# Branch merge and output projection on 1024 result rows, with split one-pass products in place of fp32 products

## The chip, the cores and the metric

The kernel runs on one core of a Trainium2 chip. The metric is the device time of one execution in microseconds (us); lower is better. Matrix products run on TensorE (PE), which has a weight load (PEld) beside the product proper; elementwise work runs on VectorE (DVE) and ScalarE (ACT), indirect transfers are issued by GpSimd (POOL), most plain transfers by SyncE (SP).

## The reference

One transformer-like layer over 16 meta rows and 1024 sequence rows (1040 rows, width 1024). Both branches run over all 1040 rows, but the output is `h[:, N_META:]`, so behind the branches only 1024 rows count:

```python
y_rwkv = rwkv7_time_mix(...) @ w_branch_rwkv[l]
y_diff = diff_attention(...) @ w_branch_diff[l]        # its rows are normed and scaled by subln_w * 0.8
merged = gates[..., :D_MODEL] * y_rwkv + gates[..., D_MODEL:] * y_diff
h = h + merged @ w_out[l]
u2 = rms_norm(h, norm2_w[l]).reshape(-1, D_MODEL)
h = h + hierarchical_moe(u2, ...)                      # 2 of 32 experts for each row
return h[:, N_META:]
```

All data is fp32.

## The kernel before, in words

The program is a row of stages with a barrier of all engines between them: norm, projections (`project_features`, `project_heads`), attention, `rwkv`, `merge_branches`, `output_and_route`, `dispatch`, `experts`, `combine`. The two projections split each fp32 operand into a high part (a rounding to the one-pass type fp32r, written by ACT) and a low part (the rest, written by DVE) and add three products, high by high, high by low and low by high. The stages behind rwkv use plain fp32 products.

`merge_branches` first loads the attention result in ten tiles of 104 rows (`mb_o`, lines 1422 and 1427), scales each twice on DVE (1460, 1461), transposes it on PE (1482) and copies it to `mb_oT` on ACT (1441). The rwkv result comes transposed from memory in one transfer (`mb_yT`, 1423). Only when all ten tiles are copied do the products start: 8 blocks of 128 output features times 2 branches, which makes 16 units of 8 row blocks k by 4 column groups of 260, 32 products each (1493). DVE gates each unit from PSUM (1467) and adds the two branches into `mT` (1471). SP loads each unit's weights (1431) and gates (1433) while the unit before it runs.

`output_and_route` loads all of `w_out` (1532), then `x` rows, the router's weights and the norm weights, and PE waits for all of them together. Then come ten tiles of 104 rows: 16 products of 512 columns (1578), and behind each tile the routing of the tile before it: transposes (1561), a copy on ACT (1608), 8 small products (1568). ACT's copy stands behind the square and the root of the current tile in ACT's program. `dispatch` ranks the rows per expert on DVE and scatters row numbers into slots with 20 indirect transfers (1700). `experts` runs 32 experts of 128 slots each. `combine` handles ten tiles: load `h`, two gathers, two DVE steps, one store.

Order on each engine is program order; engines meet by semaphores, each wait of which is written by hand.

Of the kernel before, what the change touches and what calls it, by code (L numbers as in the profile page):

```python
# [7 lines left out]
F32 = mybir.dt.float32  # L8
# [9 lines left out]
TT = 104  # L18
# [1364 lines left out]
OVER = 2 * T // (SLOTS + 1)  # L1383
NBLK = NE + OVER
BIG = 1.0e30


def merge_branches(nc, c):

    with ExitStack() as st:  # L1390
        sb, ps, sem, begin = scope(nc, st)
        yT = sb("mb_yT", [128, KD, T])
        oT = sb("mb_oT", [128, KD, T])
        o = sb("mb_o", [TT, 2, D])
        rs = sb("mb_rs", [TT, NT * DH])
        ri = sb("mb_ri", [TT, NT * DH])
        sw = sb("mb_sw", [TT, 128])
        w = sb("mb_w", [128, 2, KD, 128])
        gt = sb("mb_gt", [128, 2, T])
        part = sb("mb_part", [128, 2, T])  # L1400
        bank = ps("mb_bank", [128, 8, 512])
        sw_in = sem("mb_sw_in")
        o_in = [sem(f"mb_o_in{s}") for s in range(2)]
        y_in = sem("mb_y_in")
        w_in = [sem(f"mb_w_in{s}") for s in range(2)]
        g_in = [sem(f"mb_g_in{s}") for s in range(2)]
        rs_done = sem("mb_rs_done")
        vec = sem("mb_vec")
        turned = sem("mb_turned")
        moved = sem("mb_moved")  # L1410
        product = [sem(f"mb_product{s}") for s in range(2)]
        opened = [sem(f"mb_opened{s}") for s in range(2)]
        gated = [sem(f"mb_gated{s}") for s in range(2)]
        summed = sem("mb_summed")
        block = begin()
        LAMBDA0 = 0.8 - 0.6

        @block.sync
        def _(sp):
            sp.dma_start(sw[:], c.diff_subln_w.to_broadcast([TT, 128])).then_inc(sw_in, 16)  # L1420
            for t in range(2):
                sp.dma_start(o[:, t, :], c.oD[t]).then_inc(o_in[t], 16)
            sp.dma_start(yT[:], c.yrT.rearrange("f p t -> p f t")).then_inc(y_in, 16)
            with sp.Fori(1, NT // 2) as i:
                for s in range(2):
                    sp.wait_ge(turned, 2 * i + s - 1 + OPEN)
                    sp.dma_start(o[:, s, :], c.oD[bass.ds(2 * i + s, 1)].rearrange("o p d -> (o p) d")).then_inc(o_in[s], 16)
            with sp.Fori(0, KD) as i:
                for s, src in enumerate((c.w_branch_rwkv, c.w_branch_diff)):
                    sp.wait_ge(product[s], i + OPEN)  # L1430
                    sp.dma_start(w[:, s], src.rearrange("o (k p) f -> p (o k) f", p=128)[:, :, bass.ds(i * 128, 128)]).then_inc(w_in[s], 16)
                    sp.wait_ge(gated[s], i + OPEN)
                    sp.dma_start(gt[:, s, :], c.pT[bass.ds(i + RT + 8 * s, 1)].rearrange("o p t -> (o p) t")).then_inc(g_in[s], 16)

        @block.scalar
        def _(act):
            nc.scalar.activation(rs[:], c.o_ms[:].rearrange("p t h -> p (t h)"), ACT.Sqrt, bias=c.eps[0:TT, :],
                                 scale=1.0 / 128).then_inc(rs_done, 1)
            with act.Fori(0, NT) as i:
                act.wait_ge(turned, i + 1 + OPEN)  # L1440
                nc.scalar.copy(oT[:, :, bass.ds(i * TT, TT)].rearrange("p (b k) t -> p b k t", b=2),
                               bank[:, 0:2, 0:4 * TT].rearrange("p b (k t) -> p b k t", k=4)).then_inc(moved, 1)
            with act.Fori(0, KD) as i:
                for s in range(2):
                    act.wait_ge(g_in[s], 16 * i + 16 + OPEN)
                    nc.scalar.activation(gt[:, s, :], gt[:, s, :], ACT.Sigmoid).then_inc(opened[s], 1)

        @block.vector
        def _(dve):
            dve.wait_ge(sw_in, 16 + OPEN)  # L1450
            dve.wait_ge(rs_done, 1 + OPEN)
            ch = Chain(dve, vec)
            ch(nc.vector.tensor_scalar(sw[:], sw[:], 1.0 - LAMBDA0, None, ALU.mult))
            ch(nc.vector.reciprocal(ri[:], rs[:]))
            with dve.Fori(0, NT // 2) as i:
                ch = Chain(dve, vec, 4 * i + 2)
                for s in range(2):
                    dve.wait_ge(o_in[s], 16 * i + 16 + OPEN)
                    o3 = o[:, s, :].rearrange("p (h d) -> p h d", h=DH)
                    ch(nc.vector.tensor_tensor(o3, o3, ri[:, bass.ds((2 * i + s) * DH, DH)].unsqueeze(2).to_broadcast([TT, DH, 128]), ALU.mult))  # L1460
                    ch(nc.vector.tensor_tensor(o3, o3, sw[:].unsqueeze(1).to_broadcast([TT, DH, 128]), ALU.mult))
            split = lambda x: x.rearrange("p (n t) -> p n t", n=NCOL)
            with dve.Fori(0, KD) as i:
                for s in range(2):
                    dve.wait_ge(product[s], i + 1 + OPEN)
                    dve.wait_ge(opened[s], i + 1 + OPEN)
                    nc.vector.tensor_tensor(split(part[:, s, :]), bank[:, 4 * s:4 * s + 4, 0:CW], split(gt[:, s, :]),
                                            ALU.mult).then_inc(gated[s], 1)
                dve.wait_ge(gated[0], i + 1 + OPEN)
                dve.wait_ge(gated[1], i + 1 + OPEN)  # L1470
                nc.vector.tensor_tensor(c.mT[:, bass.ds(i, 1), :].rearrange("p o t -> p (o t)"), part[:, 0, :], part[:, 1, :],
                                        ALU.add).then_inc(summed, 1)
                dve.wait_ge(summed, i + 1 + OPEN)

        @block.tensor
        def _(pe):
            with pe.Fori(0, NT // 2) as i:
                for s in range(2):
                    pe.wait_ge(vec, 4 * i + 2 * s + 4 + OPEN)
                    pe.wait_ge(moved, 2 * i + s + OPEN)  # L1480
                    for k in range(KD):
                        last = nc.tensor.transpose(bank[:, k // 4, (k % 4) * TT:(k % 4 + 1) * TT],
                                                   o[:, s, k * 128:(k + 1) * 128], c.ident[0:TT, 0:TT])
                    last.then_inc(turned, 1)
            pe.wait_ge(moved, NT + OPEN)
            pe.wait_ge(y_in, 16 + OPEN)
            with pe.Fori(0, KD) as i:
                for s, src in enumerate((yT, oT)):
                    pe.wait_ge(w_in[s], 16 * i + 16 + OPEN)
                    pe.wait_ge(gated[s], i + OPEN)  # L1490
                    for k in range(KD):
                        for n in range(NCOL):
                            last = nc.tensor.matmul(bank[:, 4 * s + n, 0:CW], w[:, s, k, :], src[:, k, n * CW:(n + 1) * CW],
                                                    start=(k == 0), stop=(k == KD - 1))
                    last.then_inc(product[s], 1)


def output_and_route(nc, c):

    NR = NG + NE  # L1500
    with ExitStack() as st:
# [29 lines left out]
        def _(sp):  # L1531
# [17 lines left out]
            for s in range(2):  # L1549
                sp.wait_ge(h_out[s], 16 * NT // 2 + OPEN)  # L1550
                sp.wait_ge(u_out[s], 16 * NT // 2 + OPEN)
# [668 lines left out]
```

## Time and profile before

| | us |
|---|---|
| median of 3 runs | 4256.5 (4249.66 to 4256.95) |
| profiled execution, first to last instruction (its span; no other time is given for it) | 4243.3 |
| merge: SP's first transfer of the stage to its first of the next | 288.2 |
| output and route: from there to the last routing copy | 229.0 |
| dispatch, up to the experts' first gather | 64 |
| experts | 740 |
| combine | 82 |

These five stages follow one another behind 2840 us of earlier stages, which the change leaves alone, so what one stage loses or gains goes to the span in full. TensorE is busy 82% of the span; its granted clock is 0.900 of full on average.

### The profile page before, as it was taken

How to read it: one execution, taken by the hardware profiler on the slowest of the kernel's cores; microseconds unless marked ns; L12 is line 12 of the kernel's file. 1: busy time of each engine (PE TensorE's matmuls, PEld its weight loads, DVE VectorE, ACT ScalarE, POOL GpSimd, SP SyncE). 2: the span in 40 equal slices, each digit the busy share in tenths (PEclk: the TensorE clock that was granted, in tenths of full speed). 3: DMA queues.
4: the chain of work that ended last, by engine and by line, in shares of the span. 5: the costliest groups of instructions: out<-in, count | busy, mean ns of one | idle time of the engine just before them, and what ended most of it. 6: DMA issues, size and time to landing. Idle time of an engine off the chain costs nothing. (4 is left out here: it accounts for less than half of the span.)

```text
span 4243.3 us, 55444 instructions
## 1 busy us (share of the span) xinstructions
PE 3497.8 (82%) x20377; PEld 2677.2 (63%) x20378; DVE 1476.5 (35%) x2604; ACT 1048.2 (25%) x2216; POOL 310.3 (7%) x346
## 2 busy tenths in 40 slices
PE   2999969887777739989989989958978569999990
PEld 2999966665554528888878888846844334444440
DVE  3111123311556555656556556452111200000002
ACT  3111112212444424334334334321101001111110
POOL 0000002210000020110010011010000020000001
PEclk9999989998898869989989889878989779999995
DMA  3322221212111010000000000012222448888866
GB/s 102 126 93 91 94 101 41 80 38 56 40 28 35 25 40 9 23 17 7 23 17 7 23 17 13 16 63 84 80 83 62 160 162 334 327 343 337 323 264 165
DMA packets 154135, 419.32 MB, mean 99 GB/s; under 512 B 14445, under 2 KB 95447, under 8 KB 141663
## 3 DMA queue, kind: packets, MB, share of 16 engines
q1 hardware_dynamic: 119146, 331.21, 22.1%
q10 hardware_dynamic: 25620, 60.39, 3.8%
q0 software_dynamic: 9184, 25.36, 2.0%
q8 instruction: 105, 1.72, 0.2%
q14 instruction: 80, 0.65, 0.0%
HBM read 335.33 MB, written 81.58 MB: 98 GB/s over the span
## 5 line engine op out<-in xcount | busy, mean ns | idle before, releaser
L565 PE MATMUL at_S<-at_k,at_q 128*104 128x512 f32 (+10 forms) x544 | 202.9, 494 | 33.9 <-DMA at_v<-s_v 18.3
L1922 PE MATMUL ex_bank<-wd,ex_hT 128*128 128x512 f32 x512 | 227.8, 598 | 1.4 <-ACT ex_hT L1965 1.4
L1898 PE MATMUL ex_bank<-wgu,ex_xT 128*128 128x512 f32 x512 | 226.7, 596 | 0.0
L236 PE MATMUL pf_acc<-uH,pf_wH 128*128 128x260 f32 x1344 | 216.5, 283 | 12.1 <-DVE pf_wL L254 12.1
L1906 PE MATMUL ex_bank<-wgu,ex_xT 128*128 128x512 f32 x512 | 225.0, 593 | 0.0
L345 PE MATMUL ph_acc<-ph_wH,uH 128*104 128x512 f32 x480 | 196.9, 410 | 26.7 <-DVE ph_wL L356 26.7
L236 PE MATMUL pf_acc<-uH,pf_wL 128*128 128x260 f32 x1344 | 217.3, 284 | 0.0
L236 PE MATMUL pf_acc<-uL,pf_wH 128*128 128x260 f32 x1344 | 216.4, 283 | 0.0
L345 PE MATMUL ph_acc<-ph_wL,uH 128*104 128x512 f32 x480 | 193.3, 403 | 0.0
L236 PEld LDWEIGHTS pf_acc<-uH,pf_wH 128*128 128x128 f32 x1344 | 185.4, 190 | 12.4 <-issue 12.4
L345 PE MATMUL ph_acc<-ph_wH,uL 128*104 128x512 f32 x480 | 192.5, 401 | 0.0
L236 PEld LDWEIGHTS pf_acc<-uH,pf_wL 128*128 128x128 f32 x1344 | 185.4, 189 | 0.0
L236 PEld LDWEIGHTS pf_acc<-uL,pf_wH 128*128 128x128 f32 x1344 | 183.8, 189 | 0.0
L1971 DVE COPY ex_y<-ex_bank 128x512 f32<-128x512 f32 x32 | 22.1, 692 | 457.8 <-PE ex_bank L1922 457.8
L938 PE MATMUL rw_bank<-rw_kr,rw_bkz 128*104 128x208 f32 x640 | 143.3, 372 | 41.5 <-DVE rw_Pend L1341 25.7
L1578 PE MATMUL or_bank<-or_wo,mT 128*104 128x512 f32 x320 | 154.8, 647 | 26.4 <-DMA or_n<-in_norm_w 26.4
L1898 PEld LDWEIGHTS ex_bank<-wgu,ex_xT 128*128 128x128 f32 x512 | 98.2, 192 | 122.8 <-issue 122.8
L1906 PEld LDWEIGHTS ex_bank<-wgu,ex_xT 128*128 128x128 f32 x512 | 97.5, 190 | 122.2 <-issue 122.2
L586 PE MATMUL at_pv<-at_v,at_aT 104*104 104x128 f32 x880 | 140.0, 306 | 41.5 <-ACT at_aT L680 40.4
L1922 PEld LDWEIGHTS ex_bank<-wd,ex_hT 128*128 128x128 f32 x512 | 94.9, 190 | 109.7 <-issue 107.0
L586 PEld LDWEIGHTS at_pv<-at_v,at_aT 104*104 104x104 f32 x880 | 117.4, 192 | 63.8 <-ACT at_aT L680 63.8
L565 PEld LDWEIGHTS at_S<-at_k,at_q 128*104 128x104 f32 x544 | 89.8, 189 | 101.4 <-issue 84.5
(341 smaller groups left out, 6943.5 us busy)
## 6 DMA issues: line engine op xcount, KB each, us to landing
wgu<-in_expert_w_gate SPq DMA_DIRECT2D x32, 2048.0 KB, 14.7
wgu<-in_expert_w_up SPq DMA_DIRECT2D x32, 2048.0 KB
wd<-in_expert_w_down SPq DMA_DIRECT2D x32, 2048.0 KB
pf_w<-in_w_in SPq DMA_DIRECT2D x44, 512.0 KB
s_pT<-pf_ev ACTq DMA_DIRECT2D x42, 520.0 KB, 2.7
s_y<-ex_y ACTq DMA_DIRECT2D x32, 512.0 KB, 11.5
rw_x<-s_pT SPq DMA_DIRECT2D x29, 520.0 KB, 4.6
ph_w<-in_w_in SPq DMA_DIRECT2D x6, 2048.0 KB
```

Of the source, the lines that this page charges most:

```text
L236: last = nc.tensor.matmul(acc[:, s, n, 0:CW], ww[:, s, k, :], uu[:, k, n * CW:(n + 1) * CW], start=(k == 0 and j == 0), stop=(k == KD - 1 ...
L345: last = nc.tensor.matmul(acc[:, slot, :], uu[:, k, t * TT:(t + 1) * TT], ww[:, b, k, :], start=(k == 0 and j == 0), stop=(k == KD - 1 and ...
L565: last = nc.tensor.matmul(S[n][:, lo:hi], q[:, s, n, t * TT:(t + 1) * TT], k[:, s, lo:hi], start=True, stop=True)
L586: last = nc.tensor.matmul(pv[:, 0:128], aT[:, (BEFORE[u] + g) % 2, (j % 4) * TT:(j % 4 + 1) * TT], v[:, s, j, :], start=(j == 0), stop=(j ...
L938: last = mm(bank[0:TT, h, 2 * j * TT:(2 * j + 2) * TT].rearrange("p (a t) -> p a t", a=2), bkz[:, z, h, j, chunk(t)], kr[:, z, :, chunk(t) ...
L1578: last = nc.tensor.matmul(bank[0:TT, 2 * (t % 2) + n, :], c.mT[:, k, t * TT:(t + 1) * TT], wo[:, k, n * 512:(n + 1) * 512], start=(k == 0) ...
L1898: last = nc.tensor.matmul(bank[:, GATE_BANK[s], :], xT[:, s, k, :], wgu[:, s, 0, k, :], start=(k == 0), stop=(k == KD - 1))
L1906: last = nc.tensor.matmul(bank[:, UP_BANK, :], xT[:, s, k, :], wgu[:, s, 1, k, :], start=(k == 0), stop=(k == KD - 1))
L1922: last = nc.tensor.matmul(bank[:, 5 + o, :], hT[:, k, :], wd[:, s, k, o * 512:(o + 1) * 512], start=(k == 0), stop=(k == FK - 1))
L1971: copy(y[:, s, o * 512:(o + 1) * 512], bank[:, 5 + o, :]).then_inc(y_moved[o], 1)
```

## The change

In `merge_branches` and `output_and_route` each fp32 operand is split into a high and a low part of type fp32r, and each fp32 product becomes three one-pass products of up to 512 columns (`three`). The rows are the 1024 result rows alone: 2 column groups of 512 in the merge, 8 tiles of 128 rows from the output projection on, in `dispatch` (16 indirect scatters) and in `combine` too; `OVER`, the number of spare expert blocks, goes from 16 to 15. The transposes of the attention tiles stand between the units of the rwkv branch, which now all come first (`AFTER` says which tiles follow which unit). The rwkv result comes in 8 transfers, the subln weight is applied in the copy behind the transpose. `w_out` is loaded and split during the 8 units of the attention branch, into the space of the rwkv result. Loops are written out.

```diff
-OVER = 2 * T // (SLOTS + 1)
+OVER = 2 * SEQ // (SLOTS + 1)
+TS = 128
+NS = SEQ // TS
+def three(nc, out, aH, aL, bH, bL, first, last):
+    nc.tensor.matmul(out, aH, bH, start=first, stop=False)
+    nc.tensor.matmul(out, aL, bH, start=False, stop=False)
+    return nc.tensor.matmul(out, aH, bL, start=False, stop=last)
...
 def merge_branches(nc, c):
+        AFTER = ((0,), (1,), (2, 3), (4,), (5, 6), (7,), (8, 9), ())
...
+            load_w(0)
+            for k in range(KD):
+                sp.dma_start(c.mT[:, k, :], c.yrT[k, :, META:]).then_inc(y_in[k], 16)
+            load_w(1)
+            sp.dma_start(sw[:], c.diff_subln_w.rearrange("o d -> d o")).then_inc(sw_in, 16)
+            load_o(0)
+            load_o(1)
+            load_g(0)
+            load_g(1)
+            for q in range(NU):
+                if q < KD:
+                    for t in AFTER[q]:
+                        if t + 2 < NT:
+                            load_o(t + 2)
+                else:
+                    load_wo(q - KD)
+                if q + 2 < NU:
+                    load_w(q + 2)
+                    load_g(q + 2)
...
         @block.tensor
+            def unit(q):
+                aH, aL = (yH, yL) if q < KD else (oH, oL)
+                pe.wait_ge(w_low, q + 1 + OPEN)
+                if q >= 2:
+                    pe.wait_ge(gated, q - 1 + OPEN)
+                if q == KD:
+                    pe.wait_ge(o_low, NT + OPEN)
+                for k in range(KD):
+                    if q == 0:
+                        pe.wait_ge(y_low, k + 1 + OPEN)
+                    for n in range(2):
+                        cols = slice(n * 512, (n + 1) * 512)
+                        last = three(nc, bank[:, 2 * (q % 2) + n, :], wH[:, q % 2, k, :], wL[:, q % 2, k, :],
+                                     aH[:, k, cols], aL[:, k, cols], k == 0, k == KD - 1)
+                last.then_inc(product, 1)
+            for q in range(NU):
+                unit(q)
+                if q < KD:
+                    for t in AFTER[q]:
+                        turn(t)
...
         @block.scalar
+            w_split(0)
+            for k in range(KD):
+                act.wait_ge(y_in[k], 16 + OPEN)
+                nc.scalar.copy(yH[:, k, :], c.mT[:, k, :]).then_inc(y_high, 1)
+                if k == 3:
+                    w_split(1)
+            open_gate(0)
...
 def output_and_route(nc, c):
-            pe.wait_ge(w_in, 64 + OPEN)
-            for t in range(NT):
+            for t in range(NS):
+                pe.wait_ge(m_low, t + 1 + OPEN)
                 if t >= 2:
                     pe.wait_ge(added, t - 1 + OPEN)
-                for n in range(2):
-                    for k in range(KD):
-                        last = nc.tensor.matmul(bank[0:TT, 2 * (t % 2) + n, :], c.mT[:, k, t * TT:(t + 1) * TT],
-                                                wo[:, k, n * 512:(n + 1) * 512], start=(k == 0), stop=(k == KD - 1))
+                for k in range(KD):
+                    for n in range(2):
+                        cols = slice(n * 512, (n + 1) * 512)
+                        last = three(nc, bank[:, 2 * (t % 2) + n, :], mH[:, t % 2, k, :], mL[:, t % 2, k, :],
+                                     woH[:, k, cols], woL[:, k, cols], k == 0, k == KD - 1)
                 last.then_inc(product, 1)
                 if t >= 1:
                     route(t - 1)
...
 def dispatch(nc, c):
-            for t in range(NT):
+            for t in range(NS):
                 for j in range(2):
                     if t >= 1:
                         pool.wait_ge(scattered[j], 16 * t)
                     pool.indirect_dma_start(c.slotD, bass.IndirectOffsetOnAxis(ap=c.sidx[:, j, t:t + 1], axis=0),
                                             tid[:, t:t + 1], None).then_inc(scattered[j], 16)
```

On SP, the start of the merge stage before the change; `s_yrT` and `s_o` are the results of rwkv and attention in memory:

```order
-L1420 DMA mb_sw<-in_diff_subln_w 104x128
-L1422 DMA mb_o<-s_o 104x1024 x2
-L1423 DMA mb_yT<-s_yrT 128x8x1040
-L1424 UNCONDITIONAL_BRANCH
-L1424 ISA
-L1427 ISA
-L1427 DMA mb_o<-s_o 104x1024
```

and the same place after it:

```order
141 L1441 DMA mb_w<-in_w_branch_rwkv 128x8x128
142 L1461 DMA mT<-s_yrT 128x1024 x8
143 L1441 DMA mb_w<-in_w_branch_rwkv 128x8x128
144 L1463 DMA mb_sw<-in_diff_subln_w 128x1
145 L1451 DMA mb_stage<-s_o 104x1024 x2
146 L1446 DMA mb_gt<-s_pT 128x1024 x2
147 L1451 DMA mb_stage<-s_o 104x1024
148 L1441 DMA mb_w<-in_w_branch_rwkv 128x8x128
```

The first unit's weights and the eight parts of the rwkv result now come first; the second unit's weights stand behind all eight.

On ACT, the start of the merge stage after the change (`wideH` is the high part of the rwkv result, `mb_wH` that of the weights, `mb_oH` that of the attention result):

```order
797 L1526 ACTIVATE mb_rs<-o_ms,eps 104x80
798 L1533 CAST mb_wH<-mb_w 128x1024
799 L1553 CAST wideH<-mT 128x1024 x4
800 L1533 CAST mb_wH<-mb_w 128x1024
801 L1553 CAST wideH<-mT 128x1024 x4
802 L1537 ACT_TABLE_LOAD
803 L1537 ACTIVATE mb_gt<-mb_gt 128x1024
804 L1543 ACTIVATE mb_oH<-mb_bank,mb_sw 128x8x88
```

The split of the second unit's weights stands between the fourth and the fifth part of the rwkv result; before the change ACT had only the copies behind the transposes here.

On ACT, the start of the output stage after the change:

```order
850 L1757 CAST or_mH<-mT 128x1024 x3
851 L1773 ACTIVATE or_sq,or_ms<-or_h 128x1024
852 L1775 ACT_TABLE_LOAD
853 L1775 ACTIVATE or_rs<-or_ms,eps 128x1
854 L1757 CAST or_mH<-mT 128x1024
855 L1773 ACTIVATE or_sq,or_ms<-or_h 128x1024
856 L1775 ACTIVATE or_rs<-or_ms,eps 128x1
857 L1762 COPY or_uT<-or_bank 128x1024
858 L1764 COPY logits<-or_bank 128x36
```

A cast of the tile two ahead now stands ahead of each square; the copy behind the transposes (L1762) still stands behind the root of the current tile, as before.

## Rows read from the trace of the kernel before

**Rows 1.** The page's first line.

```profile
span 4243.3 us, 55444 instructions
```

**Rows 2.** Busy time by stage; columns: stretch, length, engines (times), clock, DMA share, GB/s.

```profile
2839.00:2897.00 58.00, 16.45 (x80) 13.28 (x80) 25.38 (x22) 9.10 (x12) 0.00 (x0) 0.50 0.60 184
3150.00:3359.00 209.00, 180.79 (x560) 85.04 (x560) 26.73 (x30) 25.10 (x51) 0.00 (x0) 0.90 0.21 57
3359.00:3421.00 62.00, 3.16 (x8) 2.12 (x8) 19.39 (x61) 1.73 (x3) 22.05 (x30) 0.50 0.50 204
3430.00:4170.00 740.00, 709.94 (x1918) 339.87 (x1916) 63.47 (x96) 86.89 (x129) 51.04 (x65) 0.98 0.77 302
4170.00:4244.00 74.00, 0.00 (x0) 0.00 (x0) 25.69 (x20) 0.00 (x0) 16.27 (x16) 0.50 0.77 210
```

**Rows 3.** Timeline of the merge's products; columns: start, length, engine, line, operands, count.

```profile
3011.00 14.19 PE L1493 MATMUL mb_bank<-mb_yT,mb_w 128*128 128x260 f32 x64
3025.03 14.19 PE L1493 MATMUL mb_bank<-mb_oT,mb_w 128*128 128x260 f32 x64
```

**Rows 4.** Timeline of TensorE in the head projection: fp32r products of 512 columns.

```profile
960.23 0.39 PE L345 MATMUL ph_acc<-ph_wH,uH 128*104 128x512 f32 x1
...
965.76 0.39 PE L345 MATMUL ph_acc<-ph_wH,uH 128*104 128x512 f32 x1
```

**Rows 5.** Timeline of TensorE in the feature projection: fp32r products of 260 columns.

```profile
299.52 0.64 PE L236 MATMUL pf_acc<-uL,pf_wH 128*128 128x260 f32 x4
...
326.41 0.64 PE L236 MATMUL pf_acc<-uH,pf_wH 128*128 128x260 f32 x4
```

**Rows 6.** Timeline of the merge's start and end.

```profile
2840.17 0.33 SPq L1420 DMA_DIRECT2D mb_sw<-in_diff_subln_w  x1
...
2850.60 36.40 SPq L1427 DMA_DIRECT2D mb_o<-s_o  x8
...
2862.06 1.22 DVE L1460 TENSOR_TENSOR mb_o<-mb_o,mb_ri 104x1024 f32<-104x1024 f32 x1 [10.67 <-DMA mb_o<-s_o]
...
3123.42 1.24 DVE L1467 TENSOR_TENSOR mb_part<-mb_bank,mb_gt 128x1040 f32<-128x1040 f32 x1 [12.79 <-PE mb_bank L1493]
```

**Rows 7.** The tile mb_yT: issue to landing of its one transfer.

```profile
DMA to landing us min/median/max: 18.5/18.5/18.5
```

**Rows 8.** The tile mb_w: issue to landing of a unit's weights.

```profile
DMA to landing us min/median/max: 3.8/4.1/7.8
```

**Rows 9.** Groups by line: the splits of one 128 x 1024 block.

```profile
L254 DVE TENSOR_TENSOR pf_wL<-pf_w,pf_wH 128x1024 fp32r<-128x1024 f32 x44 | 53.9, 1225 | 257.2 <-ACT pf_wH L249 257.2
L249 ACT CAST pf_wH<-pf_w 128x1024 fp32r<-128x1024 f32 x44 | 46.3, 1052 | 233.8 <-DVE pf_ev L280 214.2 <-DMA pf_w<-in_w_in 16.1 <-ACT pf_ev L262 3.5
```

**Rows 10.** Timeline of the output stage.

```profile
3128.37 0.38 SPq L1532 DMA_DIRECT2D or_wo<-in_w_out  x1
...
3149.81 29.25 PE L1578 MATMUL or_bank<-or_wo,mT 128*104 128x512 f32 x64 [26.43 <-DMA or_n<-in_norm_w]
...
3184.52 15.22 PE L1578 MATMUL or_bank<-or_wo,mT 128*104 128x512 f32 x32
...
3221.94 0.88 PE L1561 MATMUL or_bank<-ident,or_u 104*128 104x104 f32 x8
...
3330.92 15.40 PE L1578 MATMUL or_bank<-or_wo,mT 128*104 128x512 f32 x32
...
3357.39 0.19 ACT L1610 COPY logits<-or_bank 104x36 f32<-104x36 f32 x1 [3.08 <-PE or_bank L1568]
```

**Rows 11.** Timeline of dispatch: first and last of the 20 scatters.

```profile
3385.30 1.05 POOL L1700 DMA_INDIRECT s_slot<-di_tid,sidx  x1 [22.29 <-DVE sidx L1787]
...
3414.28 0.99 POOL L1700 DMA_INDIRECT s_slot<-di_tid,sidx  x1 [0.30 <-issue]
```

**Rows 12.** Timeline of the end of experts and of combine.

```profile
4146.19 0.35 ACTq L1976 DMA_DIRECT2D s_y<-ex_y  x1
...
4161.65 71.00 SPq L2058 DMA_DIRECT2D co_h<-s_h  x10
```

More of the change, by code:

```diff
@@ L1421, in _, with load_w @@
[L1421 to L1433, printed above, removed]
+            def load_w(q):
+                src = (c.w_branch_rwkv, c.w_branch_diff)[q // KD]
+                if q >= 2:
+                    sp.wait_ge(w_low, q - 1 + OPEN)
+                i = q % KD
+                sp.dma_start(w[:, q % 2], src.rearrange("o (k p) f -> p (o k) f", p=128)[:, :, i * 128:(i + 1) * 128]).then_inc(w_in[q % 2], 16)
@@ L1438, in _, with w_split @@
                                  scale=1.0 / 128).then_inc(rs_done, 1)
[L1439 to L1446, printed above, removed]
+            def w_split(q):
+                act.wait_ge(w_in[q % 2], 16 * (q // 2 + 1) + OPEN)
+                if q >= 2:
+                    act.wait_ge(product, q - 1 + OPEN)
+                nc.scalar.copy(wH[:, q % 2], w[:, q % 2]).then_inc(w_high, 1)
@@ new lines, in o_split, with wo_split @@
+            def o_split(t):
+                dve.wait_ge(o_high, t + 1 + OPEN)
+                dst, src = o_views(t, oL)
+                high, _ = o_views(t, oH)
+                for b in range(2):
+                    last = nc.vector.scalar_tensor_tensor(out=dst[:, b], in0=src[:, b], scalar=sw[:], in1=high[:, b],
+                                                          op0=ALU.mult, op1=ALU.subtract)
+                last.then_inc(o_low, 1)
+            def wo_split(k):
+                dve.wait_ge(wo_high, k + 1 + OPEN)
+                tt(yL[:, k, :], stage[:, k % 2, :], yH[:, k, :], ALU.subtract).then_inc(wo_low, 1)
@@ new lines, in gate @@
+            def gate(q):
+                i = q % KD
+                dve.wait_ge(product, q + 1 + OPEN)
+                dve.wait_ge(opened, q + 1 + OPEN)
+                src = bank[:, 2 * (q % 2):2 * (q % 2) + 2, :]
+                g = gt[:, q % 2, :].rearrange("p (n t) -> p n t", n=2)
+                split = lambda x: x.rearrange("p (n t) -> p n t", n=2)
+                if q < KD:
+                    tt(split(c.mT[:, i, :]), src, g, ALU.mult).then_inc(gated, 1)
+                else:
+                    if q > KD:
+                        dve.wait_ge(summed, i + OPEN)
+                    tt(split(part[:]), src, g, ALU.mult).then_inc(gated, 1)
+                    dve.wait_ge(gated, q + 1 + OPEN)
+                    tt(c.mT[:, i, :], c.mT[:, i, :], part[:], ALU.add).then_inc(summed, 1)
@@ L1462, in _ @@
[L1462 to L1480, printed above, removed]
-                    for k in range(KD):
[L1482 to L1495, printed above, removed]
+            nc.vector.reciprocal(ri[:], rs[:]).then_inc(ri_done, 1)
@@ L1498, in output_and_route @@
+            dve.wait_ge(ri_done, 1 + OPEN)
+            o_norm(0)
+            o_norm(1)
+            for q in range(NU):
+                if q < KD:
+                    for t in AFTER[q]:
+                        o_split(t)
+                        if t + 2 < NT:
+                            o_norm(t + 2)
+                else:
+                    wo_split(q - KD)
+                gate(q)
+                if q + 2 < NU:
+                    w_split(q + 2)
 def output_and_route(nc, c):
@@ L2054, in _ @@
         def _(sp):
-            for t in range(NT):
+            for t in range(NS):
                 if t >= 2:
@@ L2070, in _ @@
         def _(dve):
[L2071 removed]
+            for t in range(NS):
                 s = t % 2
```

280 lines of the change are left out of this document (178 added, 102 removed).

## The prediction

> **What bounds the kernel now.** I read the busy times by stage first. Stages are separated by barriers, so each has its own bound. The reader should see four things [rows 2]. In the first 58 us of the merge TensorE is busy for 16 us: the attention tiles are scaled, transposed and copied before any product runs. Between 3150 and 3359 us TensorE is busy 181 of 209 us, at 0.90 of its clock. In dispatch nothing is dense. The experts are bound by TensorE (710 of 740 us), and combine by transfers and their latency (DMA share 0.77). Between 2897 and 3128 us, left out there, one merge unit follows another without a gap: 14.03 us from start to start [rows 3]. So the merge's products, its head, and the whole output stage are on the path.
>
> **Cost of a product.** A unit of fp32 products is 64 records of two passes each, 14.03/64 = 219.2 ns for 520 columns, which is 520 columns at the 2.4 GHz level plus 2.5 ns. By that an output tile (32 records of 1024 columns) is 13.73 us. The new products are fp32r. The nearest row is the head projection, the same type and the same 512 columns: 24 of them take 5.53 us, 230.4 ns each [rows 4]. It has a stationary of 104 columns where the new ones have 128; the feature projection has 128, but 260 columns: 224 products in 26.89 us, 120.0 ns [rows 5]. Scaled by columns that gives 236 ns; the fp32 records' rate would give 216 ns. I take 230.4: a unit or a tile of 48 is 11.06 us. The bounds over all 1152 new products are -17 us and +6 us.
>
> The Trainium skill (TensorE: Matmul & The Clock Gate, Back-to-back issue gap) puts one product at its columns over 2.4 GHz plus 2.5 ns, 215.8 ns here, and a stream that alternates weight loads and products at about 131 ns for 512 columns. With 215.8 the sum below would come out 17 us lower, at about 4071. The fp32 rows agree with its formula, the fp32r rows [rows 4, 5] do not, and no row shows anything near 131.
>
> **Merge, 288.2 us now** (2840.17 to 3128.37) [rows 6, 10]. Removed: the head, in which no product runs, and one of two DVE passes per tile. Added: splits on ACT (1.05 us) and DVE (1.23 us) for each 128 x 1024 block [rows 9]. Relative to the stage's first issue:
> - The first unit's weights take about 4.1 us to land [rows 8], then come eight parts of 0.52 MB, about 1.8 us apart. Split high, split low: TensorE starts at about 9 us, at the lower clock, and reaches the fourth part at about 14 to 17 us.
> - ACT splits the second unit's weights between parts four and five, and SP issues them behind all eight parts. The trace of before shows what a transfer does there: the third attention tile, issued at 2850.60 behind the big rwkv transfer (18.5 us [rows 7]), landed at 2862.06, after 11.5 us [rows 6]. That is 21.9 us after the stage's first issue for about 5.6 MB; the 5.24 MB up to the second weights I put at 20 us. So parts five to eight wait for it, though they have long landed. Behind it stand five DVE splits, 20 + 1.1 + 5 x 1.26 = 27.4 us, and TensorE's last four row blocks. First unit done at 32 us (29 if TensorE only follows the splits, 34 if it stays at the lower clock).
> - 15 units of 11.06: 165.9 us. In them ten groups of eight transposes; such a group takes 0.88 us behind a product [rows 10]; with the changeover 1.0, 10 us. Handovers 0.5.
> - End: gate, sum, barrier as before, 3123.42 to 3128.37 [rows 6, 10], 5.0 us.
>
> Sum 213.4, **74.8 us less**. What hides the rest: per unit ACT has a weight cast, a gate and at most two tile copies (about 4 us), DVE a gate, a weight split, and at most two tile norms with splits (about 8 us), all below 11.06. The tightest are units 4 and 6, after which DVE handles two tiles whose loads are only issued when the transposes are done: from the unit's end 2 us transposes, 4 us load, a norm, a split, a gate, a weight split end at about 11.4, and TensorE needs them at 13. If loads take 2 us more, this cover is gone, and each such place costs what exceeds it. `w_out` rides under units 8 to 15.
>
> **Output, 229.0 us now** (3128.37 to 3357.39) [rows 10]. The wait for `w_out` and the small tables (first product at 3149.81, 21.4 us in) goes: TensorE now waits for one cast and one split, 2.5 us. The tables are needed only when the first product is done, 13 us later, with DVE; without the 4 MB ahead of them they are there. The first two products took 29.25 us, 1.8 above 2 x 13.73, lost at the lower clock; now 22.1 + 1.8 = 23.9. From product start to product start a tile takes (3330.92 - 3184.52)/7 = 20.91 us: 13.73 plus 7.18, of which about 5.5 is the gap in which TensorE transposes, waits for ACT's root and copy, and routes (3179.06 to 3184.52), and the rest lost clock. ACT's new cast runs beside DVE's addition, before the square, so the gap stays; 128 columns in place of 104 add 0.2. Tile period 11.06 + 7.38 = 18.44. After the last product 11.5 us (11.3 before). Sum: 2.5 + 23.9 + 5.7 + 5 x 18.44 + 12.8 + 11.5 = 148.6, **80.4 us less**. Lost clock between 0 and 3.4 us a tile bounds it at -12 and +12.
>
> **Dispatch.** The last scatter takes 0.99 us behind 0.30 us of idle, so 1.29 us each in steady flow; (3414.28 - 3385.30)/19 = 1.53 contains one early wait that stays [rows 11]. Four fewer save 5.1. DVE is busy 19.4 us there [rows 2]; a fifth fewer columns save at most 3.9, at least 0; I take 1.9. Sum **7.0**.
>
> **Experts.** Same work; weights of two experts are loaded during dispatch as before. One empty round of 16 less in the loop over spare blocks, between 0 and (4161.65 - 4146.19)/16 = 1 us [rows 12]: **0.5**.
>
> **Combine.** 81.7 us for ten tiles. By tile count it would be 16 us less, by bytes (1024 rows for 1040) 1 less. The DMA share is 0.77 [rows 2], so only the idle quarter scales with tiles: 0.2 x 19 = 4, with the bytes 5. Between 1 and 16 I take **6**, nearer to the transfers.
>
> **Sum.** 74.8 + 80.4 + 7.0 + 0.5 + 6 = 168.7. From the span of 4243.3 [rows 1]: 4074.6. The median of the runs lies 13.2 above this profiled span; with that, **4088 us**, a ratio of 0.960.
>
> **Rivals.**
> - *The second weights don't wait behind the rwkv parts.* Then unit one ends at about 22 us: **4078**. Against it, the 11.5 us of the third tile [rows 6]. The Trainium skill (DMA: Bandwidth & Descriptors, Queues, rings and completion order) says completion is not first in, first out per issuing engine, though each DMA engine takes descriptors in ring order; by the first half of that the weights could land early, by the second they can't. Chance 0.08.
> - *fp32r products at the fp32 records' rate*, 216 ns: **4071**. Against it rows 4 and 5. 0.06.
> - *The merge is paced by the reload chain, not TensorE.* SP issues a unit's weights only behind its waits for transposes and gates, and DVE serves tiles first. If each of 15 units waits 2 us: **4118**. For it: loads of 3.8 to 7.8 us [rows 8], all in one program-ordered queue; against it, a slack of 2 us at the worst unit and 5 at others. 0.12.
> - *Slower: TensorE stays at the lower level.* At 1.2 GHz 512 columns take 427 ns; 1152 x 0.197 = 227 us more, **4315**. It decides against the change from 857 of the 1152 products at that level. For it: the output stage at 0.90 of the clock and the merge's head at 0.50 [rows 2]; against it, the dense products of rows 3 and 4 run at the higher level, and the new units are as dense. 0.02.
> - The forecast, 4066 to 4112 alone: 0.71. The last 0.01: the change does its work and something else takes it back.
>
> **Range.** The terms' bounds (-17/+6, -10/+3, -12/+12, -10/+6, and 0/+30 from the chain) go together as squares to about -25 and +28 with the rivals of 4078, 4071 and part of 4118: 4060 to 4116. About 0.2% (8.5 us) is what a measurement of this kernel can tell from no change. All cases but the lower clock lie far below 4248: faster 0.97, same 0.01, slower 0.02.
>
> **What the profile would show.** Fp32r records of 512 columns 230 ns apart in merge and output. A gap of about 7 us in TensorE within the first unit, ended by a low part of the rwkv result, with the second weights' landing at about 20 us. No wait on the low part of the weights or on gates between units. First output product 2.5 us into its stage, tile periods of 18.4, TensorE idle behind ACT's copy as before. Sixteen scatters. The forecast is wrong if fp32r at 128 by 512 is not 230, if the units show gaps, or if combine goes by tiles.

## The result, and the profile after

Median of 4 runs 4050.5 us (4031.6 to 4068.6), before in the same set 4253.1 us (4247.8 to 4257.0): ratio 0.953, 95% interval 0.949 to 0.957. The change makes the kernel faster, as forecast, but by 202.6 us where 168.7 were, and 4050.5 lies below the range of 4060 to 4116. A second set gave 4057.6 against 4239.0, a gain of 181.3 us, ratio 0.956 (0.953 to 0.959).

The page's first line of the changed kernel, against [rows 1]:

```profile
span 4041.3 us, 54716 instructions
```

The stages, each from its first issue to the next one's (merge: first weights to the output stage's first load):

| us | before | after | gained | forecast |
|---|---|---|---|---|
| ahead of the merge | 2840.2 | 2822.2 | 17.9 | 0 |
| merge | 288.2 | 208.8 | 79.4 | 74.8 |
| output and route, to the last routing copy | 229.0 | 156.6 | 72.4 | 80.4 |
| dispatch | 64.3 | 57.6 | 6.7 | 7.0 |
| experts, to the last `s_y` | 724.5 | 724.6 | -0.1 | 0 |
| from there to combine | 15.5 | 14.9 | 0.6 | 0.5 |
| combine | 81.7 | 56.5 | 25.2 | 6 |

The first row is no work of the change, which leaves these stages alone; the last experiments return to it. Busy time by stage, columns as in [rows 2]:

```profile
2822.00:2880.00 58.00, 44.46 (x194) 35.49 (x195) 25.65 (x27) 21.24 (x22) 0.00 (x0) 0.84 0.61 188
3034.00:3188.00 154.00, 132.07 (x576) 110.71 (x574) 28.64 (x31) 27.93 (x47) 0.00 (x0) 0.84 0.23 83
3188.00:3245.00 57.00, 2.77 (x8) 2.27 (x8) 17.36 (x59) 1.72 (x3) 18.00 (x26) 0.50 0.55 222
3246.00:3970.00 724.00, 710.89 (x1920) 340.02 (x1920) 63.48 (x96) 86.84 (x129) 49.09 (x63) 0.99 0.77 306
3985.00:4041.00 56.00, 0.00 (x0) 0.00 (x0) 20.38 (x16) 0.00 (x0) 15.98 (x16) 0.50 0.83 300
```

Read the first line: in the merge's first 58 us TensorE is busy 44 us, before 16. The second: in the output stage it is busy 86% of the time at 0.84 of its clock, before at 0.90. The last two figures of the last line are the surprise: at nearly the same DMA share (0.83 against 0.77) combine moves 300 GB/s, before 210.

The merge's start and end in the timeline (start, length, then in brackets the idle time before and what ended it):

```profile
2829.62 0.77 PE L1394 MATMUL mb_bank<-wideH,mb_wH 128*128 128x512 f32 x1 [17.35 <-DVE wideL L1613]
...
2839.76 1.04 ACT L1533 CAST mb_wH<-mb_w 128x1024 fp32r<-128x1024 f32 x1 [6.14 <-DMA mb_w<-in_w_branch_rwkv]
...
2843.25 0.79 PE L1394 MATMUL mb_bank<-wideH,mb_wH 128*128 128x512 f32 x1 [5.91 <-DVE wideL L1613]
...
2850.71 0.88 PE L1503 MATMUL mb_bank<-ident,mb_stage 104*128 104x104 f32 x8
2851.36 0.48 PE L1394 MATMUL mb_bank<-wideH,mb_wH 128*128 128x512 f32 x1
...
3023.66 0.40 PE L1396 MATMUL mb_bank<-mb_oL,mb_wH 128*128 128x512 f32 x1
...
3025.76 0.40 PE L1396 MATMUL mb_bank<-mb_oL,mb_wH 128*128 128x512 f32 x1
3026.19 1.23 DVE L1606 TENSOR_TENSOR mb_part<-mb_bank,mb_gt 128x1024 f32<-128x1024 f32 x1 [7.58 <-PE mb_bank L1396]
```

The gap in the first unit is there as forecast: ScalarE sat 6.14 us before its cast of the second weights, ended by their DMA, 17.5 us after the first issue (2822.23) where the forecast said 20; TensorE idled 5.91 us and finished the unit at 28.5 where it said 32. The two rows at 3023.66 and 3025.76 are nine products apart, 233 ns each. Besides 2829.62 and 2843.25 TensorE has no row with idle time in the whole merge.

One output tile:

```profile
3097.46 1.03 PE L1700 MATMUL or_bank<-ident,or_u 128*128 128x128 f32 x8
3101.39 2.02 PE L1708 MATMUL or_bank<-or_wr,or_uT 128*128 128x36 f32 x16 [2.90 <-issue]
3103.22 0.78 PE L1394 MATMUL or_bank<-wideH,or_mH 128*128 128x512 f32 x1
...
3105.51 0.63 PE L1396 MATMUL or_bank<-wideL,or_mH 128*128 128x512 f32 x1
3105.93 0.63 PE L1394 MATMUL or_bank<-wideH,or_mH 128*128 128x512 f32 x1
...
3108.29 0.39 PE L1394 MATMUL or_bank<-wideH,or_mH 128*128 128x512 f32 x1
...
3115.55 0.39 PE L1396 MATMUL or_bank<-wideL,or_mH 128*128 128x512 f32 x1
3115.78 1.03 PE L1700 MATMUL or_bank<-ident,or_u 128*128 128x128 f32 x8
3118.61 0.99 ACT L1762 COPY or_uT<-or_bank 128x1024 f32<-128x1024 f32 x1
3119.71 1.67 PE L1708 MATMUL or_bank<-or_wr,or_uT 128*128 128x36 f32 x9 [2.90 <-issue]
```

After the 5.8 us of transposes, waiting and routing products, products come about 427 ns apart (3105.51 to 3105.93), the 1.2 GHz level, for about 3.5 us, and then 227 ns (3108.29 to 3115.55: 32 steps). The transposes end at 3116.8, but ScalarE's copy starts at 3118.61, behind its cast, square and root.

The tile shown is one of the short ones. VectorE adds h to the second and to the last tile at

```profile
3057.79 1.23 DVE L1740 TENSOR_TENSOR or_h<-or_bank,or_h 128x1024 f32<-128x1024 f32 x1 [5.29 <-PE or_bank L1396]
...
3174.08 1.23 DVE L1740 TENSOR_TENSOR or_h<-or_bank,or_h 128x1024 f32<-128x1024 f32 x1 [14.04 <-PE or_bank L1396]
```

which makes six periods of 19.38 us on average: four of 19.9 and two of 18.3. The gap from the transposes to the next product is 5.8 to 6.9 us, 6.3 on average, and 7 to 13 slow products follow it, which lose 1.5 to 2.7 us, 2.1 on average.

### The profile page after: what moved, and what is told of

Read it like the earlier page. It is cut to its first block and busy times, and to the rows that moved or that the text cites. A ratio compares the mean times of both kernels' runs of the same rounds, so it can differ in the third digit from the quotient of the medians.

```text
span 4041.3 us, 54716 instructions
## 1 busy us (share of the span) xinstructions
PE 3377.1 (84%) x20137; PEld 2631.2 (65%) x20138; DVE 1507.2 (37%) x2642; ACT 1075.8 (27%) x2239; POOL 302.7 (7%) x338
## 5 line engine op out<-in xcount | busy, mean ns | idle before, releaser
L565 PE MATMUL at_S<-at_k,at_q 128*104 128x512 f32 (+10 forms) x544 | 201.5, 491 | 34.7 <-DMA at_v<-s_v 19.3
L254 DVE TENSOR_TENSOR pf_wL<-pf_w,pf_wH 128x1024 fp32r<-128x1024 f32 x44 | 53.9, 1225 | 255.9 <-ACT pf_wH L249 255.9
## 6 DMA issues: line engine op xcount, KB each, us to landing
wgu<-in_expert_w_gate SPq DMA_DIRECT2D x32, 2048.0 KB, 13.2
```

The costliest lines, as they stand in the source:

```text
L254: nc.vector.tensor_tensor(wL[:, s], w[:, s], wH[:, s], ALU.subtract).then_inc(low[s], 1)
L565: last = nc.tensor.matmul(S[n][:, lo:hi], q[:, s, n, t * TT:(t + 1) * TT], k[:, s, lo:hi], start=True, stop=True)
```

## The experiments

**Combine: how long does a tile of R rows take?** The call `combine(nc, c)` stands eight times more, with R rows per transfer.

```
-                sp.dma_start(h[:, t % 2, :], c.h2D[t])
+                sp.dma_start(h[0:RH, t % 2, :], c.h2D[t, 0:RH])      # gathers, stores and DVE alike
+                combine(nc, c, 'cb', 104, 104)                       # and 112, 96, 120, ...
```

(The remarks behind # are notes of this text; the gathers, the stores and VectorE's steps are cut to R rows in the same way.)

> The changed kernel with its combine stage run again, eight more times behind the first, each time behind a barrier, over the same 8 tiles but with the first R rows of each: R = 128, 104, 112, 96, 120 for all transfers; then 104 for h and out with 128 for the gathers; then 128 for h and out with 104 for the gathers; then 128 again. Stages with R below 128 leave the other rows out. Theory 'a transfer of 104 rows is badly spread over the DMA engines': 128, 112 and 96 take 56.5 us times R/128 or a bit more (57, 51, 46), 104 and 120 take longer than 128, near the 8.2 us a tile of the kernel before: about 65. Rival 'round trips set the time, so it goes by tiles': all take about 57 us, whatever R is, and the 25 us came from ten tiles becoming eight and from nothing else, about 12 us of them unexplained. Rival 'by bytes': 104 rows take about 47 us; then something else slowed the stage before (where its tiles lie in memory, or its shorter last store).

Measured, stage to stage: 128 rows 57.2 us, 104 65.8, 112 62.5, 96 55.7, 120 67.3, 104 for h and out with 128 for the gathers 63.5, the reverse 63.3, 128 again 54.8. Windows of this kernel, 128, 104, 112, 96, 120 rows:

```profile
4054.00:4110.00 56.00, 0.00 (x0) 0.00 (x0) 20.50 (x16) 0.00 (x0) 16.00 (x16) 0.50 0.84 300
4111.20:4176.00 64.80, 0.00 (x0) 0.00 (x0) 20.56 (x16) 0.00 (x0) 16.46 (x16) 0.50 0.79 210
4177.00:4238.00 61.00, 0.00 (x0) 0.00 (x0) 20.61 (x16) 0.00 (x0) 15.31 (x16) 0.50 0.86 241
4239.50:4294.00 54.50, 0.00 (x0) 0.00 (x0) 20.49 (x16) 0.00 (x0) 14.58 (x16) 0.50 0.85 231
4295.20:4361.00 65.80, 0.00 (x0) 0.00 (x0) 20.55 (x16) 0.00 (x0) 15.82 (x16) 0.50 0.88 239
```

Eight tiles of 104 rows take 8.6 us longer than eight of 128, with 19% fewer bytes. 8.2 us a tile times ten is 82, the 81.7 of before (two later profiles of before have 88.5 and 83.9). So the gain has two parts: about 16 us from two tiles fewer (82 to 65.8) and about 9 from tiles of 128 rows in place of 104 (65.8 to 57.2). The rivals 'by tiles' (57 for all) and 'by bytes' (47 for 104) fall. But my theory that rows in multiples of 16 are cheap fails too: 112 rows take 62.5 us where it wanted 51, and 96 take 55.7 where it wanted 46.

**The transfers alone.** Stages with nothing but 16 loads of R rows (then 8 stores), and 16 gathers.

```
+                for t in range(16):
+                    sp.dma_start(h[lo:lo + R, t, :], c.h2D[t % 8, 0:R]).then_inc(h_in, 16)
```

> The changed kernel with thirteen stages behind it that only move data: 16 loads of R rows of 4 KB in one queue (and then 8 stores), R = 128, 104, 112, 96, 120 and 64 on partitions 0 up, 64 on partitions 32 to 95, 32 on partitions 0 up; then 16 gathers of 128, 104, 96 and 64 rows; then 128 rows loaded again. Combine showed 210 GB/s for 104 rows, 231 for 96 and 300 for 128 at nearly the same DMA share. Theory 'a transfer is as slow as its fullest group of partitions': 128 rows run near 420 GB/s (20 us), 96 and 64 rows from partition 0 take about the same 20 us, though they carry less, 64 rows on partitions 32 to 95 take about 10 to 12 us, 32 rows 10; 104, 112 and 120 rows take 20 us or more. Rival 'it goes by the number of DMA engines that divide the rows': 128, 112, 96, 64 and 32 rows all run at one rate, so 20, 17.5, 15, 10 and 5 us, and only 104 (13 engines) and 120 (15) are slower, 20 us each, wherever the rows lie. Rival 'single transfers are not slow, only the mix in combine is': every stage goes by its bytes near 420 GB/s. The Trainium skill (DMA: Bandwidth & Descriptors, How many engines (k)) says that a transfer is split over the largest number up to 16 that divides its rows: 13 engines for 104 rows, 16 for 128, 112, 96 and 64, which is the first rival's rule. The Trainium skill (SBUF — State Buffer, the DMA port swizzle) says that partitions 0 to 63 lie on half of the 16 ports, which is the first theory's rule.

The loads, in the order 128, 104, 112, 96, 120, 64 on partitions 0 to 63, 64 on 32 to 95, 32; the last line is 16 gathers of 104 rows:

```profile
4040.10:4063.50 23.40, 0.00 (x0) 0.00 (x0) 0.00 (x0) 0.00 (x0) 0.00 (x0) 0.50 0.91 359
4076.10:4110.50 34.40, 0.00 (x0) 0.00 (x0) 0.00 (x0) 0.00 (x0) 0.00 (x0) 0.50 0.79 198
4124.80:4152.00 27.20, 0.00 (x0) 0.00 (x0) 0.00 (x0) 0.00 (x0) 0.00 (x0) 0.50 0.95 270
4166.70:4190.90 24.20, 0.00 (x0) 0.00 (x0) 0.00 (x0) 0.00 (x0) 0.00 (x0) 0.50 0.95 260
4204.30:4239.40 35.10, 0.00 (x0) 0.00 (x0) 0.00 (x0) 0.00 (x0) 0.00 (x0) 0.50 0.91 224
4253.80:4277.20 23.40, 0.00 (x0) 0.00 (x0) 0.00 (x0) 0.00 (x0) 0.00 (x0) 0.50 0.88 179
4290.10:4304.50 14.40, 0.00 (x0) 0.00 (x0) 0.00 (x0) 0.00 (x0) 0.00 (x0) 0.50 0.82 291
4312.20:4324.40 12.20, 0.00 (x0) 0.00 (x0) 0.00 (x0) 0.00 (x0) 0.00 (x0) 0.50 0.83 173
...
4360.70:4398.50 37.80, 0.00 (x0) 0.00 (x0) 0.00 (x0) 0.00 (x0) 15.48 (x16) 0.50 0.85 180
```

Look at the length and the last figure. 128, 96 and 64 rows from partition 0 take the same 23 to 24 us: the rate falls from 359 to 260 to 179 GB/s. The same 64 rows on partitions 32 to 95 take 14.4. So for 64 rows the partitions that they lie on decide, as the first theory said, and the number of DMA engines alone doesn't. The Trainium skill (SBUF — State Buffer, Door 1: The DMA port swizzle) says that a partition's port follows from its number, with 0 to 63 on the eight even ports; the trace agrees: its 196 GB/s for 64 partitions are 179 here. Neither rule gives the other counts: 112 rows take 27.2 us, and 104 and 120 rows take 34 to 35, longer than 128. The Trainium skill (DMA: Bandwidth & Descriptors, Why a DMA increments its semaphore by 16 and not by 1) puts 104 rows on 13 DMA engines and 120 on 15; the trace agrees: the 16 loads of 104 rows have 208 packets under 512 B, 13 a load, those of 120 rows 240, 15 a load, and those of 128, 112, 96 and 64 rows 256, 16 a load. But the count doesn't price it: 13 engines with 8 rows each, or 15 with 8, carry what each of 16 carries for 128 rows, so by the count alone all three would take 23.4 us. What costs the other 11 to 12 us, no run tells. Gathers of 128 rows took 28.3 us, of 104 38.5, of 96 30.9.

**The same rows in two pieces.** `for lo, hi in ((0, 96), (96, 104))` in place of one transfer of 104.

> The changed kernel with nine stages behind it, each of 16 tile loads, all on partitions 0 up, where the same rows are moved by one transfer or by two: 128; 104; 104 as 96 and 8; 104 as 64 and 40; 128 as 64 and 64; 120 as 96 and 24; 96 as 64 and 32; 128 as 96 and 32; 8 alone. Loads alone took 23.4 us for 128 rows, 24.2 for 96, 34.4 for 104 and 35.2 for 120, and 64 rows took 23.4 on partitions 0 to 63 but 14.4 on 32 to 95. Theory 'how a transfer of 104 rows is cut over the DMA engines costs the 10 us, not the partitions that it touches': 104 as 96 and 8 takes 25 to 28 us, 120 as 96 and 24 below 30. Rival 'the partitions 96 to 103 cost it': 104 takes 33 us or more however it is cut. 128 as 64 and 64 takes 24 us if the two halves run beside each other, more if one follows the other (2 x 23.4).

Windows for 128; 104; 104 as 96 and 8; 104 as 64 and 40; 128 as 64 and 64:

```profile
4060.70:4084.20 23.50, 0.00 (x0) 0.00 (x0) 0.00 (x0) 0.00 (x0) 0.00 (x0) 0.50 0.90 357
4084.20:4120.10 35.90, 0.00 (x0) 0.00 (x0) 0.00 (x0) 0.00 (x0) 0.00 (x0) 0.50 0.77 190
4120.10:4152.50 32.40, 0.00 (x0) 0.00 (x0) 0.00 (x0) 0.00 (x0) 0.00 (x0) 0.50 0.89 210
4152.50:4189.20 36.70, 0.00 (x0) 0.00 (x0) 0.00 (x0) 0.00 (x0) 0.00 (x0) 0.50 0.78 186
4189.20:4229.50 40.30, 0.00 (x0) 0.00 (x0) 0.00 (x0) 0.00 (x0) 0.00 (x0) 0.50 0.94 208
```

My theory falls: cutting buys back 3.5 us at best, and 120 as 96 and 24, 35.2 us, gains nothing. Two halves of 64 rows (40.3) nearly follow one another instead of sharing the time of one whole (23.5). The rival (33 or more however cut) is near, but isn't shown either (32.4 as 96 and 8), since cutting has a price of its own: 96 rows as 64 and 32 take 29.8 us where 96 whole took 24.2, and 128 as 96 and 32 take 35.2 where 128 whole take 23.5. Of all these ways to move 104, 120 or 128 rows only the whole transfer of 128 is fast.

**Combine with four buffers**: `t % 2` becomes `t % 4` in its four engines' loops.

> Combine of the changed kernel with four buffers in place of two. 16.8 MB at 420 GB/s, the highest rate seen in combine, are 40 us; it takes 56.5. If round trips between the store of one tile and the load that reuses its buffer hold it up: 46 to 50 us. If the 16 DMA engines are the limit, since they are busy 0.84 of the time: 54 or more.

46.0 us, 10.5 less than the profile of the changed kernel and outside the 54.6 to 57.6 that this stage takes in nine profiles: round trips held the stage up, though the engines showed a share of 0.83.

```profile
3993.00:4039.00 46.00, 0.00 (x0) 0.00 (x0) 20.49 (x16) 0.00 (x0) 16.67 (x16) 0.50 0.92 365
```

**The second weights, two ways.** First their split moved, then their transfer.

```
             for k in range(KD):
                 act.wait_ge(y_in[k], 16 + OPEN)
                 nc.scalar.copy(yH[:, k, :], c.mT[:, k, :]).then_inc(y_high, 1)
-                if k == 3:
-                    w_split(1)
+            w_split(1)                              # VectorE alike
```

> The split of the merge's second weights on ScalarE and VectorE moved from between the fourth and fifth rwkv part to behind the eighth; the transfers stay in their order. If the 5.9 us gap in the first unit is only the wait placed there: the gap goes, TensorE follows the splits, the unit ends 6 to 7 us earlier (at about 22 us from the stage's first issue in place of 28.5) and the merge takes 202.5 us. If the second unit then waits for its weights (landing at 17.5, split 2.3): at most 1 us is given back. If the parts themselves land late: the gap stays, in part.

```
             load_w(0)
+            load_w(1)
             for k in range(KD):
                 sp.dma_start(c.mT[:, k, :], c.yrT[k, :, META:]).then_inc(y_in[k], 16)
-            load_w(1)
```

> The transfer of the merge's second weights issued ahead of the eight rwkv parts; its split stays between the fourth and fifth. If the transfers are served in the order of issue: the weights land at about 6 us instead of 17.5, each part lands about 1.3 us later, TensorE starts about 1.3 us later, and in the gap only the split itself stays, 1 to 1.5 us; the first unit ends 4 us earlier than 28.5 and the merge takes about 204.5 us. If transfers share the queue freely: TensorE starts no later.

TensorE's first product and the transposes behind the first unit, in the first kernel and in the second:

```profile
2836.27 0.77 PE L1394 MATMUL mb_bank<-wideH,mb_wH 128*128 128x512 f32 x1 [17.69 <-DVE wideL L1612]
2849.64 0.94 PE L1503 MATMUL mb_bank<-ident,mb_stage 104*128 104x104 f32 x8 [0.32 <-DVE mb_stage L1578]
```

```profile
2849.00 0.77 PE L1394 MATMUL mb_bank<-wideH,mb_wH 128*128 128x512 f32 x1 [19.26 <-DVE wideL L1613]
2863.09 0.88 PE L1503 MATMUL mb_bank<-ident,mb_stage 104*128 104x104 f32 x8
```

Between the first product and these transposes no row has idle time any more. The first unit ends 21.1 us after the stage's first issue (2828.5) in the first, 23.4 (2839.7) in the second, for 28.5; the merge takes 201.5 and 203.7 for 208.8. With the weights ahead TensorE starts 1.9 us later, as transfers served in order of issue want it. Both expectations held to about 1 us (merge 202.5 and 204.5 expected, unit ends 22 and 24.5): the gap was a wait for the landing order, placed in the middle of the splits.

**Routing off the path.** TensorE's transposes of tile t-1 stand behind the fourth row block of tile t:

```
                 for k in range(KD):
                     ...
+                    if k == 3 and t >= 1:
+                        turn(t - 1)          # the eight transposes, split off route
                 last.then_inc(product, 1)
```

ScalarE keeps tile t-1's logits and then copies tile t's transposes, behind its square and root.

> Output stage of the changed kernel with the routing taken off the path: the transposes of tile t-1 stand in the middle of the product of tile t, ScalarE copies them while the second half runs, and the routing products follow the product at once. Theory 'the 7.4 us between two products are transposes, ScalarE's queue (cast, square, root, copy) and routing products, and the clock falls behind the wait': a tile costs 11 + 1.0 + 2.0 = 14 us plus at most 0.5, the stage 2.4 + 22.5 + 6 x 14.3 + 3 + 11.5 = 125 us where it was 156.6. Rival 'the lower clock stays whatever the gap is': 1.6 us a tile more, 135. Rival 'VectorE and the transfers of h and u set the tile': no change below 17 us a tile, 148.

```profile
3057.99 1.03 PE L1700 MATMUL or_bank<-ident,or_u 128*128 128x128 f32 x8
3064.35 1.87 PE L1711 MATMUL or_bank<-or_wr,or_uT 128*128 128x36 f32 x16
3071.63 1.03 PE L1700 MATMUL or_bank<-ident,or_u 128*128 128x128 f32 x8
3077.99 1.87 PE L1711 MATMUL or_bank<-or_wr,or_uT 128*128 128x36 f32 x16
```

No idle time and, from the second tile on, no lower level: the period is 13.64 us in every one of them (48 x 0.227 + 0.9 + 1.9), for 19.4 on average, and the stage takes 120.8 us for 156.6. That is 4 us less than the theory's 125, and both rivals (135, 148) fall.

**The output products left in fp32**, on 128-row tiles, with `w_out` loaded at the stage's start: `three(...)` becomes `matmul(bank[...], c.mT[:, k, tile], wo[:, k, cols])`.

> Output stage of the changed kernel with one fp32 product in place of the three split ones, on 128-row tiles, w_out loaded again at the stage's start as before the change; casts and splits stay. If the split is worth what the forecast put it at (13.73 against 11.06 us a tile): a tile period of 21.1 to 22 where the changed kernel has 19.5, and with the load of w_out in front (19 us) a stage of 156.6 + 8 x 2.5 + 19 = 196 us. If most of the output stage's gain is tiles (ten to eight) and the load of w_out, this splits the 72 us gained into about 33 for tiles, 19 for the load and 20 for the split.

192.3 us from the load of `w_out` on, where 196 were expected. VectorE adds h to the second and to the last tile at

```profile
3112.30 1.22 DVE L1743 TENSOR_TENSOR or_h<-or_bank,or_h 128x1024 f32<-128x1024 f32 x1 [8.14 <-PE or_bank L1722]
...
3244.67 1.22 DVE L1743 TENSOR_TENSOR or_h<-or_bank,or_h 128x1024 f32<-128x1024 f32 x1 [18.63 <-PE or_bank L1722]
```

six periods of 22.06 us; in the changed kernel they are 19.38, 2.68 less, where the forecast had 2.67. Of the 72.4 us, 35.7 come from the split and from `w_out` being there (first product 2.4 us in, here 18.1: 15.7 of them), and the other 36.7 from eight tiles in place of ten and what else the new stage does.

**How far do executions differ?** Both kernels unchanged.

> The kernel before, unchanged, profiled once more: how far do two executions of the same instructions differ ahead of the merge? The merge's first transfer was issued at 2840.2 us in the profile of before and at 2822.2 in that of after, with the same code ahead of it. If this is the scatter of one execution to the next, this one lies between 2820 and 2845, as likely near one as near the other. If the change causes it, this one lies at 2840 within 2.

> The changed kernel, unchanged, timed and profiled again. So far the same code ahead of the merge took 2802.6 to 2856.7 us in eight profiles of kernels that share it, and 2840.2 and 2846.4 in two of the kernel before, while each stage behind it repeated to about 1 us. If this is scatter of one execution to the next, the stages of this profile are again 208.8, 156.6, 57.5, 724.5 and 56 within 1 us, and only the part ahead differs; the median of its runs lies between 4040 and 4065, and the ratio to before between 0.950 and 0.957.

> The kernel before, unchanged, a third profile. If the length of the part ahead of the merge doesn't depend on which of the two kernels follows, it lies between 2803 and 2857 like the others; if the kernel before is always at 2840 to 2846, it lies there. Its combine took 81.7 and 88.5 us in two profiles; tiles of 104 rows took 8.2 us each in the stage that ran them eight times: 82 us, or up to 89 if the scatter of the second profile comes again.

In the second profile of the kernel before, the part ahead of the merge took 2846.4 us. That misses both expectations, 2820 to 2845 for scatter and 2840 within 2 for an effect of the change, and settles nothing by itself. In the changed kernel's second profile the part took 2847.4 us, and in the third profile of before 2840.9. Over ten other profiles with the changed kernel's code there it ran from 2802.6 (routing off the path) to 2856.7 (fp32 products). The two extremes, from 1018 us to the merge:

```profile
1018.00:2803.00 1785.00, 1460.34 (x11073) 1251.23 (x11073) 1054.76 (x2068) 710.24 (x1737) 138.71 (x63) 0.89 0.08 23
```

```profile
1018.00:2857.00 1839.00, 1505.77 (x11073) 1283.82 (x11073) 1060.88 (x2068) 709.12 (x1736) 136.95 (x61) 0.86 0.08 22
```

The same 11073 matmuls are busy 45 us longer at a granted clock of 0.86 in place of 0.89; VectorE and ScalarE do the same work in the same time. What sets the granted clock of an execution, no run tells. Everything behind repeats to about 1.5 us: in the changed kernel's second profile merge 207.9, output 156.7, dispatch 57.3, experts 723.2; before 288.3, 229.2 to 229.5, 64.1, 724.5. Only combine scatters: 81.7, 88.5, 83.9 before, 56.5 and 56.7 after, and 54.6 to 57.6 over all nine profiles whose first combine is that of after. The third profile of before fits both of its expectations, and doesn't tell them apart; three of before (mean 2842.5) and eleven with the code of after (mean 2833.1) leave a few us open, but the second set's runs differ by 181.3 us and the stages from the merge on by 188.4 (1406.3 against 1217.9), so in that set nothing is left that the change would have to give ahead of the merge. In the first set, 202.6 us, 14.2 are left.

**All three edits together**: split last, routing inside, four buffers.

> The changed kernel with the three edits that shortened a stage: the second weights' split behind the last rwkv part (merge 208.8 to 201.5), the routing inside the next tile's product (output 156.6 to 120.8), four buffers in combine (56.5 to 46.0). If the stages add up as they did so far, a span's stages from merge on are 7.3 + 35.8 + 10.5 = 53.6 us shorter than the changed kernel's, 1165 us in place of 1219, and the median is about 3997 us, 0.941 of before. If they take something from one another (the output stage now ends with the same transfers in less time, dispatch starts on a busier queue), dispatch or the merge shows it, up to 5 us.

Median of 6 runs 3996.3 us (3978.2 to 4022.8) where about 3997 were expected, ratio to before 0.942 (0.939 to 0.946); 1164.8 us from the merge on (1165 expected). The merge takes 200.7, output 121.4, combine 45.7: they add up, and dispatch gives back 0.3.

## Why the prediction was right or wrong

**Wrong: combine.** The step "By tile count it would be 16 us less, by bytes (1024 rows for 1040) 1 less" and behind it "only the idle quarter scales with tiles". It gained 25.2 in this pair of profiles and 28.7 on the means (84.7 over three profiles of before, 56.0 over the nine of after). The step took the busy share of 0.77 as transfers that run at their rate, so that time could only follow bytes or tiles. The row had the answer in its last column: 210 GB/s at a share of 0.77, where the experts' row beside it has 302 at the same 0.77 [rows 2]. A tile of 104 rows costs 8.2 us and one of 128 7.1, so both the count and the price fall: 82 to 57. Neither bound allowed for a price that falls with more rows. Why a transfer of 104 rows is slower than one of 128 stays open.

**Wrong: the base.** The sum was made from one profile plus 13.2 us. Runs of the changed kernel lie 37 us apart (granted clock 0.911 in the two fastest, 0.903 in the slowest); the profiles put such differences ahead of the merge. Of the 37.3 us between the sum and 4050.5, 19.7 are stages (188.4 in place of 168.7, by the means above), 3.4 a median of before that was lower in this set, and the other 14.2 how four runs fell, which is luck. By the stages alone the median would have been 4068, inside the range; the second set's median lies 7.0 above what the same 188.4 would give. Nor was the 13.2 an offset: a run's own time is 1.7 us above its span (4042.96 and 4041.3 in the profile shown), the rest was one execution against others. The range of 28 us each way had no term for this. With combine put at 25 us the sum would have been 4069, and 4050.5 within 28 us of it: the time left the range because both misses went the same way.

**Right in kind, off in size: output, 8 us less gained.** First product 2.4 us in (2.5 forecast) and the split's price (2.68 for 2.67) held. The step "128 columns in place of 104 add 0.2. Tile period 11.06 + 7.38 = 18.44" failed: 19.38. The products were even cheaper (227 ns for 230, 0.2 us a tile), but the gap was 6.3 us where the step had 5.7, and the slow products behind it lost 2.1 where it had 1.7. In the gap the 16 routing products took 1.8 to 3.0 us, with no gap 1.7; the transposes took 1.03 either way. That is 0.94 us a period, 5.6 over six, and the tail took 13.7 us for 11.5. The rows of before had one lost clock for 13.7 us of product, and I carried it to 11. That the split's price held to 0.01 is partly luck: the product fell by 0.16 us more than forecast, and gap and lost clock grew by as much.

**Right: merge, 4.6 us more gained.** The second weights behind the rwkv parts, the gap, no waits between later units: all seen, and two experiments remove the gap. The wait ended 2.5 us earlier than put, the unit 3.5. A product cost 233 ns for 230.4, 2.1 us more over 15 units, and a group of transposes 0.65 (2850.71 to 2851.36) for 1.0, 3.5 less over ten.

**Right:** dispatch 6.7 (7.0), sixteen scatters; the experts unchanged.

**The rivals.** The weights landing at once, 216 ns for a product, waits between merge units and the 1.2 GHz level throughout did not occur.

## What to carry to other kernels

Read busy share and GB/s of a transfer stage together: a high share at a low rate says that the transfers are badly shaped, and 128 partitions in one transfer can be faster than 104, absolutely. Where a short wait splits a dense stream of products, add to the wait what the products behind it lose at the lower clock (here 1.5 to 2.7 us for 5.8 to 6.9); moving the dependent work into the next product's middle removed both, 35.8 us in eight tiles. And ask of several executions how far the untouched part differs before a single profile becomes the base of a sum.

## What the runs showed of the hardware, unexpected

- 16 loads of 64 rows of 4 KB took 23.4 us on partitions 0 to 63 and 14.4 on 32 to 95; 16 of 128 rows took 23.4.
- 104 and 120 rows took 34 to 35 us, with 13 and 15 DMA engines in use by their packets, and two transfers of 64 rows 40.3 where one of 128 took 23.5.
- The same 1.8 ms of instructions took 54 us more in one execution than in another, at a granted clock of 0.86 for 0.89.
